# Two logarithms behind one another on ScalarE, and two masks ahead of the next head's decays on VectorE, in a gated recurrence on one core

## The chip, the core and the metric

The kernel runs on one core of a Trainium2 chip. The metric is the device time of one execution in microseconds (us); a comparison uses the median of several runs. Two kernels are told apart when they differ by more than about 0.2% of the time.

## The reference

The program is a model of four layers on 512 tokens of width 1024: an attention layer with a short convolution, a gated recurrence, and two further layers with a feed-forward part. The change touches the gated recurrence alone. It has 8 heads and two directions (forwards and backwards), 128 keys and 128 values a head, 512 tokens behind a context of 256. Of the reference this is what it computes, cut to what matters:

```python
def forget_terms(z, lb):
    lb = jnp.clip(lb.astype(jnp.float32), 0.0, 1.0).reshape(C_HEADS, 1, C_KEY_DIM)
    log_f = jnp.logaddexp(jnp.log(lb), jnp.log1p(-lb) + jax.nn.log_sigmoid(z))
    k = (1 - lb) * jax.nn.sigmoid(-z)
    return k, log_f
...
    b = jnp.cumsum(log_f, axis=3)
    k_state = k * jnp.exp(b_last - b)
    decay = jnp.exp(b_last[:, :, :, 0, :])
...
        def step(s, xs):
            q_n, k_n, v_n, b_n, qi_n, ks_n, d_n = xs
            o_inter = jnp.einsum('bhcd,bhde->bhce', qi_n, s)
            diff = b_n[:, :, :, None, :] - b_n[:, :, None, :, :]
            w = jnp.exp(jnp.where(tri, diff, -jnp.inf))
            scores = jnp.einsum('bhcd,bhsd,bhcsd->bhcs', q_n, k_n, w)
            o_n = o_inter + jnp.einsum('bhcs,bhse->bhce', scores, v_n)
            return d_n[..., None] * s + jnp.einsum('bhcd,bhce->bhde', ks_n, v_n), o_n
```

With the inputs given here the bound `lb` is 0, so the logarithm of a decay is log_sigmoid(z). The kernel gets it as min(z, 0) - ln(1 + exp(-|z|)): an absolute value, an exponential and a logarithm on ScalarE, and the rest on VectorE.

## The kernel before

The recurrence stands in `stage_c`. Each engine has its own program there, written out by hand, and runs it strictly in order; semaphores join them. No scheduler moves anything.

**Turns.** Every engine loops over turns t = 0 to 9. In turn t the projections of head t are made (five tiles, t below 8), head h = t-1 is scanned, and head t-2 gets its last scaling. The five tiles of a turn are z of direction 0, z of direction 1, q, and then two more: i and i (the values of two heads) in an even turn, g and g (the gates of two heads) in an odd one.

**TensorE** sets the pace. In turn t it runs: `flip_keys(h)` (L1455), the first z tile, `own_states(h)` (L1468, L1471), `turn(t-2)` (L1523), the second z tile, `products(h, 0)` and `products(h, 1)` (L1495, L1502), the q tile, `chunk(h, 0)`, `products(h, 2)`, `chunk(h, 1)`, `products(h, 3)`, the fourth and the fifth tile, `chunk(h, 2)`, `chunk(h, 3)`. A `chunk` is L1512, L1513 and L1515, and only L1515 needs the masked scores of its chunk (the semaphore `summed`). A tile is made of triples L315, L316, L317, a product of operands that are split into a high and a low part.

**Weights.** A unit of weights arrives in `c_raw`. ScalarE writes its high part (L1322, in `empty`, ahead of the exponential), GpSimd then its low part (L310), and TensorE waits for that. The q tile's `empty` makes the high part of the last unit that the i tiles of an even turn need. Their first TensorE instruction is therefore behind GpSimd's L310 of that unit.

**ScalarE** in turn t: `root(t-2)`, `decay_weights(h)` (L1362), `copies(h)` (L1369, L1371), the exponentials of the query and key levels (L1407, L1409), then `empty` of the five tiles, with `key_weights(t, 0)` (L1393, L1395) behind the third and `key_weights(t, 1)` behind the fourth. `empty` of a z tile is a copy (L1332), an absolute value (L1335), the next unit's high part (L1322), an exponential (L1338) and a logarithm (L1339). An activation whose function is not in the table set that is loaded has an ACT_TABLE_LOAD ahead of it.

**VectorE** in turn t: `queries(h)` (L1202, L1203), `scale(t-2)` (L1275), `keys(h)` (L1215, L1216), `states(h)` (L1230, L1233), `weigh(h)` (L1245, L1247, L1250), `gate(t-2)` (L1285), and then for direction 0 and after it for direction 1: `decays(t, dr)` and two `masks(h, n)` (L1260 to L1266). `decays(t, dr)` waits for `absolute`, which ScalarE's logarithm raises, and its last instruction raises `exponents`; the `queries` of the next turn wait for that. `products(h, 0)` waits for `levelled`, which L1250 raises. `keys(h)` raises `levels_y`, for which ScalarE's L1409 waits.

Of the kernel before, what the change touches and what calls it, by code (L numbers as in the profile page):

```python
# [25 lines left out]
CH = 8  # L26
# [148 lines left out]
def program(nc, d):  # L175
    f32, f32r, bf16 = mybir.dt.float32, mybir.dt.float32r, mybir.dt.bfloat16
    A = mybir.ActivationFunctionType
# [3 lines left out]
    with es:  # L181
# [54 lines left out]
        def stage_sems():  # L236
            turn[0] += 1
            return sets[turn[0] % 2], sets[(turn[0] + 1) % 2]
# [835 lines left out]
        buf_t1 = [c(T), c(T)]  # L1074
# [27 lines left out]
        def stage_c():  # L1102
# [4 lines left out]
            S, N = stage_sems()  # L1107

            def rev(ap):
                return ap[:, ::-1]  # L1110
# [6 lines left out]
            def bank2(b):  # L1117
                return PS[:, b:b + 2, :].rearrange("p b n -> p (b n)")
# [10 lines left out]
            with nc.Block() as block:  # L1129
# [11 lines left out]
                def _(dve):  # L1141
                    steps = [0]

                    def link(ins):
                        steps[0] += 1
                        ins.then_inc(S.dve_step, 1)
                        dve.wait_ge(S.dve_step, steps[0])
# [14 lines left out]
                    def decays(t, dr):  # L1162

                        u = 2 * t + dr
                        z, t1, nk, b = hz[:, dr, :], buf_t1[dr], buf_nk[dr], buf_b[dr]
                        dve.wait_ge(S.absolute, u + 1)
                        if t:
                            dve.wait_ge(S.keys, u - 1)
                            dve.wait_ge(S.weights, u - 1)
                            dve.wait_ge(S.levels_y, t)  # L1170
                        nc.vector.scalar_tensor_tensor(nk, z, 0.0, t1, O.max, O.add).then_inc(S.log_k, 1)
                        dve.wait_ge(S.log_k, u + 1)
                        link(nc.vector.scalar_tensor_tensor(z, z, 0.0, t1, O.min, O.subtract))
                        if dr == 0:
                            link(nc.vector.tensor_tensor_scan(b, resets, z, 0.0, O.mult, O.add))
                        else:
                            nc.vector.tensor_tensor_scan(rev(b[:, 0:L]), resets[:, 0:L], rev(z[:, 0:L]), 0.0, O.mult,
                                                         O.add)
                            link(nc.vector.tensor_tensor_scan(rev(b[:, L:T]), resets[:, L:T], rev(z[:, L:T]), 0.0,
                                                              O.mult, O.add))  # L1180
                        link(nc.vector.tensor_tensor(t1, b, nk, O.add))
                        end = P - 1 if dr == 0 else 0
                        b4, t4 = [v[:, 0:L].rearrange("p (n c) -> p n c", c=P) for v in (b, t1)]
                        nc.vector.tensor_tensor(z[:, 0:L].rearrange("p (n c) -> p n c", c=P),
                                                b4[:, :, end:end + 1].to_broadcast([P, NB, P]), t4, O.subtract)
                        cend = T - 1 if dr == 0 else L
                        nc.vector.tensor_tensor(z[:, L:T], b[:, cend:cend + 1].to_broadcast([P, LC]), t1[:, L:T],
                                                O.subtract).then_inc(S.exponents, 1)
# [64 lines left out]
                    def masks(h, n):  # L1253

                        i = h * NB + n
                        bank = PS[:, 4 + i % 2, :]
                        dve.wait_ge(S.products, i + 1)
                        if i >= 2:
                            dve.wait_ge(S.chunk_out, i - 1)
                        nc.vector.tensor_tensor(near_prod, bank[:, P:P + NEAR * 32], near_mask, O.mult)\  # L1260
                            .then_inc(S.tree, 1)
                        nc.vector.tensor_copy(am[i % 2], bank[:, 0:P])
                        dve.wait_ge(S.tree, i + 1)
                        link(nc.vector.tensor_reduce(near_sum, near_prod.rearrange("p (l c) -> p c l", l=NEAR), AX,
                                                     O.add))
                        nc.vector.copy_predicated(am[i % 2].rearrange("p (b c) -> p b c", b=4),  # L1266
                                                  block_mask.bitcast(mybir.dt.uint32).rearrange("p (b c) -> p b c", b=4),
                                                  near_sum.unsqueeze(1).to_broadcast([P, 4, 32])).then_inc(S.summed, 1)

                    def scale(h):  # L1270

                        dve.wait_ge(S.head_root, h + 1)
                        if h:
                            dve.wait_ge(S.head_turned, h)
                        nc.vector.tensor_tensor(scaled_o.rearrange("p (n c) -> p n c", n=NB),  # L1275
                                                PS[:, 7, :].rearrange("p (n c) -> p n c", n=NB),
                                                ssq[:, 2, h, :].unsqueeze(2).to_broadcast([P, NB, P]), O.mult)\
                            .then_inc(S.head_copied, 1)
# [9 lines left out]
                    for t in range(CH + 2):  # L1288
                        h = t - 1
                        if 0 <= h < CH:  # L1290
                            queries(h)
                        if t >= 2:
                            scale(t - 2)
                        if 0 <= h < CH:
                            keys(h)
                            states(h)
                            weigh(h)
                        if t >= 2:
                            gate(t - 2)
                        for dr in range(2):  # L1300
                            if t < CH:
                                decays(t, dr)
                            if 0 <= h < CH:
                                masks(h, 2 * dr)
                                masks(h, 2 * dr + 1)

                @block.scalar
                def _(act):
                    steps = [0]

                    def link(ins):
                        steps[0] += 1
                        ins.then_inc(S.act_step, 1)
                        act.wait_ge(S.act_step, steps[0])
# [9 lines left out]
                    def empty(i):  # L1324

                        t, (kind, j) = i // 5, C_TILES[i % 10]
                        ps = bank2(2 * (i % 2))
                        act.wait_ge(S.pe_tile, i + 1)
                        if kind == "z":
                            if t:  # L1330
                                act.wait_ge(S.flipped, 3 * t)
                            nc.scalar.activation(hz[:, j, :], ps[:, 0:T], A.Copy)  # L1332
                            if t:
                                act.wait_ge(S.levels_y, t)
                            nc.scalar.activation(buf_t1[j], ps[:, 0:T], A.Abs).then_inc(S.act_out, 1)  # L1335
                            high([10 * (t // 2) + u for u in SPLIT_AFTER[i % 10]])
                            act.wait_ge(S.act_out, i + 1)
                            link(nc.scalar.activation(buf_t1[j], buf_t1[j], A.Exp, scale=-1.0))  # L1338
                            nc.scalar.activation(buf_t1[j], buf_t1[j], A.Ln, bias=1.0).then_inc(S.absolute, 1)  # L1339
                            return  # L1340
                        if kind == "q":
                            if t >= 2:
                                act.wait_ge(S.products, NB * (t - 1))
                            ins = nc.scalar.activation(hq[t % 2], ps[:, 0:L], A.Silu)
                        elif kind == "g":
                            ins = nc.scalar.activation(yh[:, t - 1 + j, :], ps[:, 0:L], A.Silu)
                        else:
                            p_ = t // 2
                            if p_ >= 2:
                                act.wait_ge(S.chunk_out, NB * 2 * (p_ - 1))  # L1350
                            n = 4 if j == 0 else 2
                            ins = nc.scalar.activation(hi[p_ % 2][:, 4 * j:4 * j + n, :],
                                                       ps[:, 0:n * 256].rearrange("p (i n) -> p i n", i=n), A.Copy)
                        ins.then_inc(S.act_out, 1)
                        high([10 * (t // 2) + u for u in SPLIT_AFTER[i % 10]])
# [1550 lines left out]
        S, N = stage_sems()  # L2906
# [188 lines left out]
```

## Time and profile before

| what | value |
| --- | --- |
| median of 3 runs | 2624.97 us (2623.14 to 2625.95) |
| profiled execution, its own time | 2623.78 us |
| its span, first to last instruction | 2622.0 us |
| TensorE busy over the span | 2365.1 us (90%) |
| VectorE busy | 1457.2 us (56%) |
| ScalarE busy | 1097.0 us (42%) |
| GpSimd busy | 157.8 us (6%) |
| mean granted TensorE clock | 0.954 |

Times in the trace are counted from the span's start. The recurrence lies between about 560 and 1017 us. A row of a timeline gives the start, the duration, the engine, the line, the operation and its tiles; brackets at its end hold the idle time of that engine ahead of the instruction and what ended it. An instruction that waits for something while it already counts as started shows a longer duration instead.

### The profile page before, as it was taken

How to read it: one execution, taken by the hardware profiler on the slowest of the kernel's cores; microseconds unless marked ns; L12 is line 12 of the kernel's file. 1: busy time of each engine (PE TensorE's matmuls, PEld its weight loads, DVE VectorE, ACT ScalarE, POOL GpSimd, SP SyncE). 2: the span in 40 equal slices, each digit the busy share in tenths (PEclk: the TensorE clock that was granted, in tenths of full speed). 3: DMA queues.
4: the chain of work that ended last, by engine and by line, in shares of the span. 5: the costliest groups of instructions: out<-in, count | busy, mean ns of one | idle time of the engine just before them, and what ended most of it. 6: DMA issues, size and time to landing. Idle time of an engine off the chain costs nothing. (4 is left out here: it accounts for less than half of the span.)

```text
span 2622.0 us, 36224 instructions
## 1 busy us (share of the span) xinstructions
PE 2365.1 (90%) x15406; PEld 1926.5 (73%) x15406; DVE 1457.2 (56%) x2166; ACT 1097.0 (42%) x1738; POOL 157.8 (6%) x70
## 2 busy tenths in 40 slices
PE   6699988948999987799899999999898899999998
PEld 3598856737888876477578888886676578888875
DVE  0413276266787965436756666536536666666344
ACT  1311165155686673413734333334325724334243
POOL 0100001032232220000000000000000000000000
PEclk7799989979999997899999999999999999999999
DMA  9411100011111111222021322222130012222212
GB/s 400 152 58 56 64 1 17 1 48 50 41 57 50 57 51 39 103 112 81 1 76 49 112 97 97 103 99 80 49 145 33 2 65 81 96 97 97 104 65 80
DMA packets 34529, 201.01 MB, mean 77 GB/s; under 512 B 3776, under 2 KB 5312, under 8 KB 14656
## 3 DMA queue, kind: packets, MB, share of 16 engines
q1 hardware_dynamic: 34368, 198.69, 21.1%
q8 instruction: 122, 2.00, 0.3%
q14 instruction: 39, 0.32, 0.0%
HBM read 196.58 MB, written 2.10 MB: 76 GB/s over the span
## 5 line engine op out<-in xcount | busy, mean ns | idle before, releaser
L315 PE MATMUL ps<-a_high,w_high 128*128 128x512 f32 (+1 forms) x1680 | 628.1, 374 | 33.0 <-DVE a_low L2051 22.7
L317 PE MATMUL ps<-a_high,w_low 128*128 128x512 f32 (+1 forms) x1680 | 619.7, 369 | 0.0
L316 PE MATMUL ps<-a_low,w_high 128*128 128x512 f32 (+1 forms) x1680 | 619.7, 369 | 0.0
L1673 DVE TENSOR_TENSOR w_low<-raw_ring,w_high 128x2048 fp32r<-128x2048 f32 x102 | 233.8, 2292 | 282.6 <-ACT w_high L1667 277.8
L315 PEld LDWEIGHTS ps<-a_high,w_high 128*128 128x128 f32 x1680 | 319.0, 190 | 94.9 <-DVE w_low L1673 17.2
L316 PEld LDWEIGHTS ps<-a_low,w_high 128*128 128x128 f32 x1680 | 319.4, 190 | 53.6 <-issue 1.9
L317 PEld LDWEIGHTS ps<-a_high,w_low 128*128 128x128 f32 x1680 | 319.4, 190 | 52.4
L1667 ACT ACTIVATE w_high<-raw_ring 128x2048 fp32r<-128x2048 f32 x102 | 195.3, 1914 | 368.6 <-PE ps L317 283.3
L315 PE MATMUL ps<-c_high,c_w_high 128*128 128x512 f32 (+1 forms) x448 | 167.2, 373 | 45.6 <-POOL c_w_low L310 42.4
L315 PE MATMUL ps<-x_high,ab_high 128*128 128x256 f32 (+1 forms) x528 | 180.6, 342 | 27.4 <-POOL x_low L331 27.2
L316 PE MATMUL ps<-x_low,ab_high 128*128 128x256 f32 (+1 forms) x528 | 179.4, 340 | 0.0
L317 PE MATMUL ps<-x_high,ab_low 128*128 128x256 f32 (+1 forms) x528 | 178.9, 339 | 0.0
L316 PE MATMUL ps<-c_low,c_w_high 128*128 128x512 f32 (+1 forms) x448 | 164.0, 366 | 0.0
L317 PE MATMUL ps<-c_high,c_w_low 128*128 128x512 f32 (+1 forms) x448 | 163.9, 366 | 0.0
L315 PEld LDWEIGHTS ps<-x_high,ab_high 128*128 128x128 f32 x528 | 101.1, 191 | 41.6 <-issue 26.5
L315 PEld LDWEIGHTS ps<-c_high,c_w_high 128*128 128x128 f32 x448 | 86.8, 194 | 60.7 <-POOL c_w_low L310 43.8
L310 POOL TENSOR_TENSOR c_w_low<-c_raw,c_w_high 128x1024 fp32r<-128x1024 f32 x42 | 111.6, 2663 | 311.1 <-ACT c_w_high L1322 311.1
L2840 DVE TENSOR_TENSOR arena<-ps,arena 128x1024 f32<-128x1024 f32 x44 | 53.8, 1224 | 134.4 <-PE ps L317 134.3
L310 DVE TENSOR_TENSOR ab_low<-ab_raw,ab_high 128x2048 fp32r<-128x2048 f32 x17 | 39.0, 2292 | 135.9 <-ACT ab_high L303 135.8
L317 PEld LDWEIGHTS ps<-x_high,ab_low 128*128 128x128 f32 x528 | 101.1, 191 | 11.1
L316 PEld LDWEIGHTS ps<-x_low,ab_high 128*128 128x128 f32 x528 | 101.3, 192 | 10.2
L317 PEld LDWEIGHTS ps<-c_high,c_w_low 128*128 128x128 f32 x448 | 86.4, 193 | 13.6
(338 smaller groups left out, 4033.5 us busy)
## 6 DMA issues: line engine op xcount, KB each, us to landing
raw_ring<-w_dram SPq DMA_DIRECT2D x112, 1024.0 KB, 4.9
ada_ring<-w_dram SPq DMA_DIRECT2D x24, 1024.0 KB, 18.0
c_raw<-wc_dram SPq DMA_DIRECT2D x48, 512.0 KB, 3.5
ab_raw<-w_dram SPq DMA_DIRECT2D x17, 1024.0 KB, 4.9
x<-xT_dram SPq DMA_DIRECT2D x1, 2048.0 KB, 22.6
out_dram<-x SPq DMA_DIRECT2D x1, 2048.0 KB, 7.2
arena<-r_dram SPq DMA_DIRECT2D x2, 992.0 KB, 7.2
raw_cb<-cb_dram SPq DMA_DIRECT2D x1, 1280.0 KB, 15.2
```

Source lines behind the costliest of these rows:

```text
L310: (nc.gpsimd if by_pool else nc.vector).tensor_tensor(self.low(n), self.raw(n), self.high(n).bitcast(f32), O.subtract)\
L315: nc.tensor.matmul(out, wh, xh, start=start, stop=False)
L316: nc.tensor.matmul(out, wh, xl, start=False, stop=False)
L317: return nc.tensor.matmul(out, wl, xh, start=False, stop=stop)
L1667: nc.scalar.activation(self.high(n), self.raw(n), A.Copy).then_inc(w_hi, 1)
L1673: nc.vector.tensor_tensor(self.low(n), self.raw(n), self.high(n).bitcast(f32), O.subtract)\
L2840: nc.vector.tensor_tensor(hs[:, j % 2, :, :], tile2(PAIR[j % 4]), rstd[:, 1, :].unsqueeze(1).to_broadcast([P, 2, L]), O.mult)\
```

## The change

In ScalarE's program the z tile's `empty` ends with the exponential. Behind the exponential of the second z tile stand now both logarithms, one for each direction, with one wait ahead of the two. In VectorE's program the first two masks of head h stand ahead of the decays of head t, and the decays of direction 1 follow those of direction 0 at once; masks 2 and 3 stay last. Nothing else changes: the same activations, the same vector instructions, the same matmuls and transfers.

```diff
                         for dr in range(2):
-                            if t < CH:
-                                decays(t, dr)
                             if 0 <= h < CH:
                                 masks(h, 2 * dr)
                                 masks(h, 2 * dr + 1)
+                            if t < CH and dr == 0:
+                                decays(t, 0)
+                                decays(t, 1)
...
                             act.wait_ge(S.act_out, i + 1)
-                            link(nc.scalar.activation(buf_t1[j], buf_t1[j], A.Exp, scale=-1.0))
-                            nc.scalar.activation(buf_t1[j], buf_t1[j], A.Ln, bias=1.0).then_inc(S.absolute, 1)
+                            ins = nc.scalar.activation(buf_t1[j], buf_t1[j], A.Exp, scale=-1.0)
+                            if j:
+                                link(ins)
+                                for b in buf_t1:
+                                    nc.scalar.activation(b, b, A.Ln, bias=1.0).then_inc(S.absolute, 1)
                             return
```

ScalarE in turn 1 before, from the exponential of the first z tile (L1338) to the table load ahead of the q tile (L1344); L1339 is the logarithm:

```order
L1338 ACTIVATE arena<-arena 128x768
L1339 ACT_TABLE_LOAD
L1339 ACTIVATE arena<-arena 128x768
L1332 ACTIVATE arena<-ps 128x768
L1335 ACTIVATE arena<-ps 128x768
L1322 ACTIVATE c_w_high<-c_raw 128x1024
L1338 ACT_TABLE_LOAD
L1338 ACTIVATE arena<-arena 128x768
L1339 ACT_TABLE_LOAD
L1339 ACTIVATE arena<-arena 128x768
L1344 ACT_TABLE_LOAD
```

The same place of the changed kernel, where the exponential is L1339, the logarithms are L1343 and the q tile's load is L1348:

```order
L1339 ACTIVATE arena<-arena 128x768
L1333 ACTIVATE arena<-ps 128x768
L1336 ACTIVATE arena<-ps 128x768
L1323 ACTIVATE c_w_high<-c_raw 128x1024
L1339 ACTIVATE arena<-arena 128x768
L1343 ACT_TABLE_LOAD
L1343 ACTIVATE arena<-arena 128x768 x2
L1348 ACT_TABLE_LOAD
```

Two of the four table loads are gone, the second exponential follows the weights' high part directly, and the first logarithm stands behind the second tile.

VectorE in turn 2, from the end of `weigh` (L1250) on, as the difference between the two programs; L1285 is `gate`, L1260 to L1266 are a mask, L1171 and L1173 begin the decays:

```order
 L1250 TENSOR_TENSOR arena<-arena 128x3584
 L1285 SCALAR_TENSOR_TENSOR arena<-ps,arena 128x512
+L1260 TENSOR_TENSOR arena<-ps,arena 128x192
+L1262 COPY arena<-ps 128x128
+L1264 TENSOR_REDUCE arena<-arena 128x32
+L1266 COPY_PREDICATED arena<-arena 128x128
+L1260 TENSOR_TENSOR arena<-ps,arena 128x192
+L1262 COPY arena<-ps 128x128
+L1264 TENSOR_REDUCE arena<-arena 128x32
+L1266 COPY_PREDICATED arena<-arena 128x128
 L1171 SCALAR_TENSOR_TENSOR arena<-arena 128x768
 L1173 SCALAR_TENSOR_TENSOR arena<-arena 128x768
```

The two masks have moved from behind the first direction's decays to directly behind `gate`.

## Rows read from the trace of the kernel before

**Rows 1.** For whom TensorE waited, 560 to 1010 us: total, times, longest.

```profile
PE ps L315 <- POOL c_w_low L310: 50.1, 7, 34.6
PE ps L1495 <- DVE arena L1250: 18.8, 7, 7.7
PE ps L1515 <- DVE arena L1266: 8.6, 10, 1.4
```

**Rows 2.** Timeline of TensorE, turns 0, 1, 3, 5, 6 and 7.

```profile
594.00 0.58 PE L315 MATMUL ps<-c_w_high,c_high 128*128 128x256 f32 x1 [6.78 <-POOL c_w_low L310]
...
647.01 0.49 PE L1515 MATMUL ps<-arena 128*128 128x128 f32 x2 [0.72 <-DVE arena L1266]
...
752.64 0.49 PE L1515 MATMUL ps<-x,arena 128*128 128x128 f32 x2
...
849.21 0.53 PE L1502 MATMUL ps<-arena 128*64 128x64 f32 x12
...
857.28 0.49 PE L1515 MATMUL ps<-arena 128*128 128x128 f32 x2 [1.39 <-DVE arena L1266]
...
895.96 0.62 PE L1495 MATMUL ps<-arena 128*32 128x32 f32 x48 [1.86 <-DVE arena L1250]
...
905.50 0.49 PE L1515 MATMUL ps<-arena 128*128 128x128 f32 x2 [1.43 <-DVE arena L1266]
...
907.88 0.49 PE L1515 MATMUL ps<-arena 128*128 128x128 f32 x2 [0.23 <-DVE arena L1266]
...
909.32 0.39 PE L315 MATMUL ps<-c_w_high,c_high 128*128 128x256 f32 x1
...
964.35 0.49 PE L1515 MATMUL ps<-x,arena 128*128 128x128 f32 x2 [0.23 <-DVE arena L1266]
```

**Rows 3.** Busy us of PE, PEld, DVE, ACT, POOL; granted clock; DMA (turns 3, 5).

```profile
743.00:753.00 10.00, 9.89 (x150) 8.11 (x150) 9.83 (x14) 6.97 (x8) 2.88 (x1) 0.83 0.20 54
...
847.00:857.00 10.00, 8.15 (x148) 6.73 (x148) 9.83 (x12) 8.43 (x9) 2.92 (x1) 1.00 0.19 55
```

**Rows 4.** Timeline of VectorE, turns 5 and 6.

```profile
848.18 0.94 DVE L1171 SCALAR_TENSOR_TENSOR arena<-arena 128x768 f32<-128x768 f32 x1
849.15 3.03 DVE L1173 SCALAR_TENSOR_TENSOR arena<-arena 128x768 f32<-128x768 f32 x1
...
855.94 0.35 DVE L1260 TENSOR_TENSOR arena<-ps,arena 128x192 f32<-128x192 f32 x1
...
859.54 0.95 DVE L1171 SCALAR_TENSOR_TENSOR arena<-arena 128x768 f32<-128x768 f32 x1
...
865.29 0.35 DVE L1260 TENSOR_TENSOR arena<-ps,arena 128x192 f32<-128x192 f32 x1
...
878.18 0.69 DVE L1275 TENSOR_TENSOR arena<-ps,arena 128x512 f32<-128x512 f32 x1 [3.47 <-ACT arena L1386]
...
885.45 0.29 DVE L1230 COPY x<-ps 128x128 f32<-128x128 f32 x1 [1.89 <-PE ps L1471]
...
889.71 6.10 DVE L1250 TENSOR_TENSOR arena<-arena 128x3584 f32<-128x3584 f32 x1
```

**Rows 5.** Timeline of GpSimd, turns 4, 5 and 6.

```profile
801.62 2.97 POOL L310 TENSOR_TENSOR c_w_low<-c_raw,c_w_high 128x1024 fp32r<-128x1024 f32 x1 [7.22 <-ACT c_w_high L1322]
...
848.45 2.92 POOL L310 TENSOR_TENSOR c_w_low<-c_raw,c_w_high 128x1024 fp32r<-128x1024 f32 x1 [5.81 <-ACT c_w_high L1322]
...
889.21 2.85 POOL L310 TENSOR_TENSOR c_w_low<-c_raw,c_w_high 128x1024 fp32r<-128x1024 f32 x1 [12.25 <-ACT c_w_high L1322]
...
905.28 2.38 POOL L310 TENSOR_TENSOR c_w_low<-c_raw,c_w_high 128x1024 fp32r<-128x1024 f32 x1 [5.70 <-ACT c_w_high L1322]
```

**Rows 6.** Timeline of ScalarE, turns 5 and 6.

```profile
848.39 1.28 ACT L1338 ACT_TABLE_LOAD   x1
849.68 0.85 ACT L1338 ACTIVATE arena<-arena 128x768 f32<-128x768 f32 x1
...
883.60 3.20 ACT L1409 ACTIVATE arena<-arena 128x3584 f32<-128x3584 f32 x1
```

## The prediction, as it was put on record

> **What bounds the kernel now.** I read three views, in this order. The first is the table of waits inside the recurrence [rows 1]. The low parts of the weights cost TensorE 50.1 us, of which the entry (34.6 us) and the first i tile (6.78 us [rows 2]) are most; the query levels (L1250) cost 18.8 us and the masks (L1266) 8.6 us, in ten waits. Second, TensorE's timeline: between these waits it works without a gap, so it is the engine that the turn waits for, and what is won on it is won in the end. The ten mask waits come in pairs of 1.6 to 1.95 us, in turns 1, 2, 5, 6 and 7, between the first and the last shown in [rows 2]; 1.43 and 0.23 us are the pair of turn 6. Turns 3 and 4 have none: L1515 at 752.64 us starts without idle time [rows 2]. There the granted clock is 0.83 of full speed over ten microseconds where turn 5 has 1.00 [rows 3], the q tile runs later by about 1.3 us, and the masks are there in time. Third, the timelines of VectorE, GpSimd and ScalarE show why the masks are late: they stand behind the decays of direction 0, 848.18 to 855.94 us, 7.76 us in turn 5 [rows 4].
>
> Two things in [rows 4, 5] carry the rest. L1173 takes 3.03 us where its neighbour L1171, of the same size, takes 0.94: GpSimd's L310 ran from 848.45 us for 2.92 us, and the vector instruction that reads two tensors of the on-chip memory stood still. I take 2.1 us for one such stall. And L1250 takes 6.10 us in turn 6 because L310 began at 889.21 us, half a microsecond ahead of it; that is what keeps TensorE's products waiting 1.86 us [rows 2].
>
> **The change part by part.**
>
> *The masks move forward.* In turn 5 L1171 starts at 848.18 us, and the second products have left TensorE at 849.21 + 0.53 = 849.74 us [rows 2, 4]. The four L1260 to L1266 of a mask take 1.2 us, two masks 2.4. The first ends, held by one GpSimd stall, near 851.0, the second near 852.2. TensorE asks for them at 857.28 - 1.39 = 855.9 us [rows 2], so both are 3.7 us early and both waits go: at most 8.6 us [rows 1].
>
> In even turns something else is late next. The i tile (L315 at 909.32 us) needs the low part that GpSimd makes from 905.28 us on, for 2.38 us [rows 2, 5]. Without the two waits TensorE would be there at 909.32 - 1.66 = 907.66 us, just when GpSimd is done; in turn 4 the same L310 took 2.97 us, with VectorE at work beside it [rows 5]. The gain of an even turn therefore lies between 1.66 and 1.66 - 0.59 = 1.07 us. VectorE is busy with decays there after the change, so I take 1.2, 0.45 less than the wait, in turns 2 and 6. Masks: 8.6 - 0.9 = 7.7 us. Turns 3 and 4 bring nothing, if the clock dips there again.
>
> *ScalarE's two logarithms.* Each pair saves two table loads of 1.28 us [rows 6] a turn, 16 in all. ScalarE has idle time behind the q tile in every turn, so this counts only where TensorE waits for it: in turn 0, where the i tile waits 6.78 us for a low part whose high part stands behind the q tile on ScalarE [rows 2]. Ahead of it one load goes and one logarithm of 0.85 us (as long as the exponential in [rows 6]) comes: 1.28 - 0.85 = 0.43 us. It is nothing if GpSimd falls behind a vector instruction there; I take 0.4.
>
> A rule of the Trainium skill prices this otherwise. The loads in the trace are followed by their activation after 1.29 us (848.39 to 849.68 us, [rows 6]). "ScalarE: Activation LUTs", section "What ACT_TABLE_LOAD costs", adds about 1.38 us of draining to each switch; by that the term of turn 0 would be about 1.8 us and the total 1.4 us more. The row shows no such gap.
>
> The other side: `absolute` of direction 0 comes later. ScalarE's second exponential can start at 848.39, without the load; with 0.85, 1.28 and 0.85 us behind it the first logarithm ends near 851.4 us. VectorE is through with the masks at 852.2, so this is hidden. If VectorE were through earlier it would wait for it, at no cost to TensorE.
>
> *What the decays lose.* In turn 5 they start at 852.2 instead of 848.2 us. Direction 0 takes 7.76 - 2.1 = 5.7 us without a stall, and the L310 behind the q tile gives it one; it ends near 860.2. Direction 1 takes 865.29 - 859.54 = 5.75 us [rows 4] and ends near 866. Then come two masks (2.4) with a stall (2.1) and the 14 `queries` (4.7) with another: 877.5 us. Before, `scale` could start at 878.18 us, after 3.47 us of idle time [rows 4]; with TensorE 1.64 us earlier it could at 876.5. So `scale` and `keys` come 1.0 us late against TensorE. Behind them VectorE has 1.89 us of idle time ahead of `states` [rows 4], and so 0.9 us are left: free. State keys and masks 2 and 3 keep margins of 0.9 us and more. In turns 2 to 3, 4 to 5 and 6 to 7 the scaling is later still, and there is more room.
>
> *An overtaking.* L1409 waits for `levels_y`, and with it the first z tile's copy, its high part and GpSimd's L310, which came 889.21 - 883.60 = 5.61 us after L1409's start [rows 5, 6]. If `keys` are 1.0 us late against TensorE, L310 comes 0.5 us behind the start of L1250 rather than 0.5 ahead of it, and L1250 would run its plain 3.88 us (6.10 less the stall and a little). The products' wait of 1.86 us would go; the low part, delayed behind L1250, would be ready just as the q tile wants it. That is worth about 1.7 us a turn, in turns 2 and 6 (in turn 4 nothing moves, since turn 3 gains nothing). The ends are 0 and 3.4 us. My delay of 1.0 us is a chain of a dozen sums and the point of decision 0.5 us, so I take one of the two, 1.7 us.
>
> The Trainium skill speaks for the upper end: "SBUF — State Buffer", section "SBUF: two separate sides", says that VectorE and GpSimd lock a shared pair of ports, that the one that starts first keeps it for the whole instruction, and that the other blocks fully. The stretched L1173 and L1250 agree with the half of it in which GpSimd is first. By that rule the term would be 3.4 us, and the sum 11.5.
>
> **Sum.** 7.7 + 0.4 + 1.7 = 9.8 us. The profiled execution of before took 2623.78 us for a span of 2622.0, so the changed one would take 2614.0. The median of the three runs lies 1.2 us higher than that execution: 2624.97 - 9.8 = 2615.2 us.
>
> **The rivals.**
>
> *The overtaking takes place in both turns, or the dips go too.* 7.7 + 0.4 + 3.4 = 11.5 us give 2613.5. If TensorE keeps its full clock in turns 3 and 4, 1.3 us each come on top: 2610.9. For it: the rows show no other difference between those turns and turn 5. Against it: the idle time removed stands behind the place where the clock falls.
>
> *The gain is partly given back.* One more GpSimd stall of 2.1 us in an odd turn makes `scale` 3.1 us late, 1.2 more than VectorE's room, and the products that much later, in three pairs of turns: 9.8 - 1.7 - 3.6 = 4.5 us are left, 2620.5. For it: stalls are decided by tenths. Against it: each L310 can hold VectorE only once, and I have counted all of them.
>
> *Nothing changes.* The masks stay late, because something else than the decays holds them. For it only that turns 3 and 4 have no wait; against it that TensorE asks 3.7 us after they can be done. 2625.
>
> *Slower.* VectorE gets so late in odd turns that the next `states`, L1250 and the products come late on TensorE. The place is L1230 in turns 2, 4 and 6, behind 1.89 us of room. It decides from about 3.6 us more delay per odd turn than I worked out on: 3.6 less 0.9 of room, times three turns, is 8.1 us. At 5 us it costs 12.3 and the kernel takes about 2629. Against it: it needs two further stalls in each such turn.
>
> **How the numbers follow.** The forecast with none, one or both overtakings within it (gains of 7 to 12 us) holds 0.62, the clock back as well 0.08, the gain partly given back 0.17, nothing 0.08, slower 0.05. The forecast gives 2615.2. About 0.2% (5.2 us) is what a measurement of this kernel can tell from no change. Faster by more: the first two and a third of the third case, 0.76; same: 0.18; slower: 0.06, with a chance for clock dips elsewhere. The range goes from the lowest case with a microsecond of spread between runs, 2610, to the middle of the partial case, 2622.
>
> **What would show it.** The waits of L1515 for L1266 are gone or below 1 us in total. L1171 of direction 0 starts 3 to 5 us later than before. ScalarE has 16 table loads less. In turns 2 and 6 TensorE's first i instruction waits for GpSimd by up to 1 us. L1250 takes 3.9 or 6.1 us in turns 2 and 6, which decides the overtaking. The wait of L1275 shrinks from 3.47 us to nothing in odd-to-even steps, while that of L1230 stays above 0. Wrong would make it: a wait of L1495 for L1250 above 1.9 us, new waits for L1371 or L310, or a clock below 0.95 in the recurrence.

## The result, and the profile after

The changed kernel took 2609.2 us (median of 5 runs, 2606.78 to 2612.85), the kernel before 2624.97 us (5 runs). The ratio is 0.994, with a 95% interval of 0.9927 to 0.9954: 15.8 us less, where 9.8 were forecast, and below the range's low end of 2610.0 us. Timed once more in a later run it took 2613.26 us beside 2624.93 for the kernel before, 11.7 us less, with a ratio of 0.9954 (0.994 to 0.9968). The two intervals overlap. The gain is there, and it is between 8 and 19 us.

First the page of the changed kernel: its span, and busy time, share and instructions of each engine.

```profile
span 2607.4 us, 36208 instructions
...
PE 2357.1 (90%) x15406; PEld 1921.9 (74%) x15406; DVE 1449.7 (56%) x2166; ACT 1075.9 (41%) x1722; POOL 165.3 (6%) x70
```

ScalarE has 1722 instructions instead of 1738: the 16 table loads. The table of TensorE's waits, 560 to 1000 us, answers to [rows 1]:

```profile
PE ps L315 <- POOL c_w_low L310: 51.1, 9, 34.6
PE ps L1499 <- DVE arena L1250: 17.2, 6, 8.0
```

No row is left for the masks. `products` is L1499 now and `chunk` L1516, L1517, L1519. The wait for L1250 stands in six turns instead of seven, and GpSimd is waited for nine times instead of seven.

The recurrence, from its first tile to the start of the stage behind it, takes 439.0 us instead of 454.6 in the two profiles. That is 15.6 us. The spans of the two profiled executions differ by 14.6 us (2622.0 and 2607.4): the stages around the recurrence, which the change does not touch, took 1.0 us longer in the second. Since TensorE's order is the same, the two can be laid side by side by the starts of each group of its instructions. The table was worked out so, from the starts in the two timelines of TensorE:

| part of TensorE's order | gain, us |
| --- | --- |
| `chunk(h, 0)` and `chunk(h, 1)`, turns 1, 2, 5, 6, 7 | 2.5 + 2.2 + 2.2 + 2.2 + 2.2 |
| the same, turns 3 and 4 | 0.2 + 0.2 |
| wait of the i tile for GpSimd, turns 2 and 6 | -1.3, -0.6 |
| wait of the products for L1250, turn 2 | 1.9 |
| products and q tile at another clock, turns 3, 4, 6 | 1.5 + 1.5 - 1.5 |
| first tile of turn 1 at another clock | 1.6 |
| turn 0 | 0.0 |
| behind the last tile (clock) | 0.9 |
| sum, before rounding | 15.6 |

Turns 3 and 4 show no wait for a mask in the kernel before, and still had a trace of one. The mask of turn 3 ended at 752.58 us, and L1515 started 0.30 us behind L1513 instead of 0.22, at 752.64 us ([rows 2]); no idle time stands in its row. These are the 0.2 us of the second row.

The first row is larger than the idle time that the view of waits had shown. TensorE's timeline of the kernel before, turn 5, and of the changed one at the same place shows why:

```profile
855.28 0.38 PE L1512 MATMUL ps<-x,arena 128*128 128x128 f32 x2
855.50 0.39 PE L1513 MATMUL ps<-arena 128*128 128x128 f32 x2
```

```profile
846.88 0.38 PE L1516 MATMUL ps<-x,arena 128*128 128x128 f32 x2
847.10 0.39 PE L1517 MATMUL ps<-arena 128*128 128x128 f32 x2
847.32 0.39 PE L1519 MATMUL ps<-arena 128*128 128x128 f32 x2
847.64 0.63 PE L1499 MATMUL ps<-arena 128*32 128x32 f32 x48
```

Without a wait the instructions start 0.22 us apart although each is shown with 0.39: they overlap. With one, L1515 of the kernel before ([rows 2]) started at 857.28 us, 1.78 after L1513, and the view calls 1.39 of that idle; 857.70 - 857.28 = 0.42 us passed until the next group, where it is now 0.32. So the group `chunk(h, 0)`, up to the next products, shrank from 2.42 to 0.76 us, 1.66 for an idle time of 1.39. Each of the ten waits cost 0.27 us more than its idle time, 2.7 us in all.

VectorE's timeline of the changed kernel, turn 5, answers to [rows 4]:

```profile
840.48 0.36 DVE L1260 TENSOR_TENSOR arena<-ps,arena 128x192 f32<-128x192 f32 x1 [0.63 <-PE ps L1506]
...
841.47 1.15 DVE L1266 COPY_PREDICATED arena<-arena 128x128 f32<-128x128 uint32 x1
...
843.52 0.31 DVE L1266 COPY_PREDICATED arena<-arena 128x128 f32<-128x128 uint32 x1
843.73 0.95 DVE L1171 SCALAR_TENSOR_TENSOR arena<-arena 128x768 f32<-128x768 f32 x1
...
867.60 0.69 DVE L1275 TENSOR_TENSOR arena<-ps,arena 128x512 f32<-128x512 f32 x1 [1.20 <-ACT arena L1390]
...
874.87 0.29 DVE L1230 COPY x<-ps 128x128 f32<-128x128 f32 x1 [1.56 <-PE ps L1475]
```

The products of this turn start at 839.33 us. The second mask is done 4.5 us later and the decays start 4.4 us behind the products' start, where it was 0.44 before (848.18 - 847.74): 4.0 us later, as worked out. The wait for the scaling is 1.20 us and not nothing. GpSimd's timeline says why. This L310 began during the `queries`, 14 short instructions end to end, and took 5.18 us: VectorE kept it off, and not the other way round.

```profile
863.48 5.18 POOL L310 TENSOR_TENSOR c_w_low<-c_raw,c_w_high 128x1024 fp32r<-128x1024 f32 x1 [3.13 <-ACT c_w_high L1323]
```

In turn 5 of the kernel before it was the other way round. GpSimd got in between two of the same 14 instructions, and L1203, of 0.42 us, took 2.63 (a row of GpSimd's timeline and one of VectorE's):

```profile
868.53 2.54 POOL L310 TENSOR_TENSOR c_w_low<-c_raw,c_w_high 128x1024 fp32r<-128x1024 f32 x1 [9.06 <-ACT c_w_high L1322]
868.72 2.63 DVE L1203 TENSOR_TENSOR arena<-arena 128x256 f32<-128x256 f32 x1
```

And the overtaking, in VectorE's and in GpSimd's timeline of the changed kernel, turns 2 and 6:

```profile
678.20 3.88 DVE L1250 TENSOR_TENSOR arena<-arena 128x3584 f32<-128x3584 f32 x1
...
879.13 6.10 DVE L1250 TENSOR_TENSOR arena<-arena 128x3584 f32<-128x3584 f32 x1
```

```profile
678.22 6.10 POOL L310 TENSOR_TENSOR c_w_low<-c_raw,c_w_high 128x1024 fp32r<-128x1024 f32 x1 [10.29 <-ACT c_w_high L1323]
...
878.96 2.52 POOL L310 TENSOR_TENSOR c_w_low<-c_raw,c_w_high 128x1024 fp32r<-128x1024 f32 x1 [10.30 <-ACT c_w_high L1323]
```

In turn 2 L1250 starts 0.02 us ahead of L310 and takes its plain 3.88 us, and L310 takes 6.10. In turn 6 L310 is ahead by 0.17 us, and it is the other way round.

### The profile page after: what moved, and what is told of

Read it like the earlier page. It is cut to its first block and busy times, and to the rows that moved or that the text cites. A ratio compares the mean times of both kernels' runs of the same rounds, so it can differ in the third digit from the quotient of the medians.

```text
span 2607.4 us, 36208 instructions
## 1 busy us (share of the span) xinstructions
PE 2357.1 (90%) x15406; PEld 1921.9 (74%) x15406; DVE 1449.7 (56%) x2166; ACT 1075.9 (41%) x1722; POOL 165.3 (6%) x70
## 5 line engine op out<-in xcount | busy, mean ns | idle before, releaser
L310 POOL TENSOR_TENSOR c_w_low<-c_raw,c_w_high 128x1024 fp32r<-128x1024 f32 x42 | 119.2, 2841 | 291.1 <-ACT c_w_high L1323 291.1
L310 DVE TENSOR_TENSOR ab_low<-ab_raw,ab_high 128x2048 fp32r<-128x2048 f32 x17 | 39.0, 2292 | 135.9 <-ACT ab_high L303 135.8
```

The source lines that it names most:

```text
L310: (nc.gpsimd if by_pool else nc.vector).tensor_tensor(self.low(n), self.raw(n), self.high(n).bitcast(f32), O.subtract)\
```

## The experiments

**VectorE's edit alone (e1_masks).** ScalarE's program stays that of before.

```diff
                         for dr in range(2):
-                            if t < CH:
-                                decays(t, dr)
                             if 0 <= h < CH:
                                 masks(h, 2 * dr)
                                 masks(h, 2 * dr + 1)
+                            if t < CH and dr == 0:
+                                decays(t, 0)
+                                decays(t, 1)
```

> VectorE's edit alone (the first two masks ahead of both decays), ScalarE as before with its logarithms apart. Theory A: the whole gain comes from the masks no longer standing behind the first decays; the ten waits of TensorE for L1266 go, each worth its idle time and about a quarter of a microsecond of restart, 11.6 us together, less 1 to 2 us of waiting for GpSimd in even turns. Expected 2610 to 2615 us. Theory B: the pairing of the logarithms carries a good part (table loads saved on ScalarE): then 2618 us or more.

Measured: 2614.1 us, ratio 0.9959 (0.9946 to 0.9971), in theory A's span. The waits for masks are gone from its trace, and the pairs of `chunk` take what they take in the changed kernel. Its recurrence takes 445.1 us, 6.1 more than the changed kernel's. Of that 1.9 are the overtaking of turn 2, which it misses (L310 is 0.17 us ahead there), 1.6 the first tile of turn 1, 0.7 turn 0; the rest is clock and GpSimd in even turns. Its interval and the changed kernel's overlap.

**ScalarE's edit alone (e2_logs).**

```diff
-                            link(nc.scalar.activation(buf_t1[j], buf_t1[j], A.Exp, scale=-1.0))
-                            nc.scalar.activation(buf_t1[j], buf_t1[j], A.Ln, bias=1.0).then_inc(S.absolute, 1)
+                            ins = nc.scalar.activation(buf_t1[j], buf_t1[j], A.Exp, scale=-1.0)
+                            if j:
+                                link(ins)
+                                for b in buf_t1:
+                                    nc.scalar.activation(b, b, A.Ln, bias=1.0).then_inc(S.absolute, 1)
```

> ScalarE's edit alone, VectorE as before. Theory A: the first decays now wait for a logarithm that ends some 3 us later against TensorE's products, so the masks behind them come 3 us later too: TensorE waits about 3 us more in each of 7 turns, about 20 us slower than before, some 2643 us. Theory B (saved table loads are worth something by themselves): not slower than before.

Measured: 2645.8 us, ratio 1.0076 (1.0063 to 1.0089): slower by 20 us, the time that theory A gives. From its table of TensorE's waits:

```profile
PE ps L1518 <- DVE arena L1266: 20.4, 11, 6.3
PE ps L1498 <- DVE arena L1250: 11.1, 6, 1.9
```

The waits for masks grew by 11.8 us and not by 20, and not evenly: L1518 waited 6.3 us in turn 1, 3.8 in turns 4 and 6, and in turns 2, 3, 5 and 7 about 1.0 and 0.6. The rest of the 17.4 us by which the recurrence grew is mostly a lower clock, in the products or the q tile of turns 2, 3, 5 and 7 and behind the long waits of turns 1, 4 and 6. So the cause was named and the size met in part by luck. Saving table loads is worth nothing where the result is wanted earlier. The edit is harmless only behind the masks.

**GpSimd gives way to L1250 (e3_yield).** To the changed kernel comes one wait, on a semaphore that VectorE raises just ahead of L1250.

```diff
                     for n in range(UC["c_out"] + 2):
+                        t = 2 * (n // 10) + (n % 10 == 7)
+                        if n % 10 in (2, 7) and 1 <= t < CH:
+                            pool.wait_ge(S.key_sums, t)
                         c_stream.split_low(pool, n, by_pool=True)
```

> The changed kernel, and GpSimd's low part of the unit behind the first z tile waits for key_sums, which VectorE raises just ahead of L1250. Theory A (whoever of VectorE and GpSimd starts first keeps the other off): L1250 or the L1245 ahead of it are stretched in no turn, TensorE's wait of 1.85 us for L1250 goes in the five turns that still have it, and the low part is ready about when the q tile wants it: 8 to 9 us less than the changed kernel, 2600 to 2602 us. Rival: the low part comes too late for the q tile and gives 1 to 2 us back in each turn: no gain over the changed kernel.

Measured: 2602.72 us, ratio 0.9915 (0.9902 to 0.9929), 6.5 us below the first median of the changed kernel (10.5 below its second) and a little above theory A's span. The recurrence takes 431.9 us, 7.1 less. `L1250` is L1253 here. VectorE's and GpSimd's timelines in turn 6, and the row of TensorE's waits for it:

```profile
877.14 3.88 DVE L1253 TENSOR_TENSOR arena<-arena 128x3584 f32<-128x3584 f32 x1
```

```profile
878.43 4.84 POOL L310 TENSOR_TENSOR c_w_low<-c_raw,c_w_high 128x1024 fp32r<-128x1024 f32 x1 [13.98 <-ACT c_w_high L1326]
```

```profile
PE ps L1502 <- DVE arena L1253: 8.0, 1, 8.0
```

One wait is left, that of the last turn, which has no tile to cover it. The five others took 1.93 us each with them. Some is given back: in turns 4 and 6 the i tile waits longer for GpSimd (2.3 us for `products(h, 3)` and the wait together in turns 2, 4 and 6, where the changed kernel has 2.3, 2.0 and 1.6), and behind the fourth and fifth tile of odd turns 0.5 us appear.

**The next high part ahead of the Silu (e4_high_first).** In the changed kernel, for the q tile only.

```diff
-                            ins = nc.scalar.activation(hq[t % 2], ps[:, 0:L], A.Silu)
+                            high([10 * (t // 2) + u for u in SPLIT_AFTER[i % 10]])
+                            nc.scalar.activation(hq[t % 2], ps[:, 0:L], A.Silu).then_inc(S.act_out, 1)
+                            return
```

> The changed kernel, and in the q tile's empty the high part of the next unit stands ahead of the Silu. Theory A: in even turns the fourth tile waits for that unit's low part, which comes 0.5 us earlier: about 2 us less than the changed kernel over turns 0, 2, 4, 6, some 2607 us. Rival: the turn's length is set elsewhere by then, or the low part now falls on another vector instruction: no difference.

Measured: 2611.07 us, ratio 0.995 (0.9937 to 0.9963): no difference that can be measured from the changed kernel. The profile shows where it went. Turn 0 is 2.5 us shorter (the high part also comes ahead of the Silu's table load). The i tile of turn 2 comes 1.05 us earlier against the products ahead of it, those of turns 4 and 6 only 0.2 and 0.1. The clock took 1.6 in the first tile of turn 1, and in turns 3 and 4 products and q tile ran 1.3 to 1.4 us slower each. The recurrence takes 439.7 us, 0.6 more than the changed kernel's. So the rival was right in its outcome, and in this profile the cause was the clock, which neither named.

**The kernel before with GpSimd giving way (e6_before_yield).** The edit of e3_yield, nothing else.

> The kernel before with the one addition that GpSimd waits for key_sums. Theory A: the clock falls in products and q tile only behind TensorE's wait of 1.85 us for L1250. That wait goes in turns 2 to 7 (11.6 us), so no turn dips, and turns 3 and 4 now show the pair of waits for masks that the others have (2.2 us each). The masks come no earlier against the products, so their waits grow by what the products come earlier, up to 1.9 us a turn, and eat most of the gain: between 2614 and 2625 us. Theory B (dips come anywhere, with no tie to that wait): turns 3 and 4, or others, still have a q tile of 6.9 us.

Measured: 2644.68 us, ratio 1.0077 (1.0064 to 1.009), 20 us slower, far outside what I gave. What theory A says of the q tile came out: no turn has a slow one. The rest did not. TensorE's waits, and VectorE's timeline behind L1253 in turn 5:

```profile
PE ps L1518 <- DVE arena L1269: 29.5, 7, 4.3
```

```profile
858.65 0.74 DVE L1288 SCALAR_TENSOR_TENSOR arena<-ps,arena 128x512 f32<-128x512 f32 x1
859.31 2.49 DVE L1174 SCALAR_TENSOR_TENSOR arena<-arena 128x768 f32<-128x768 f32 x1
861.83 3.19 DVE L1176 SCALAR_TENSOR_TENSOR arena<-arena 128x768 f32<-128x768 f32 x1
...
869.75 1.73 DVE L1269 COPY_PREDICATED arena<-arena 128x128 f32<-128x128 uint32 x1
```

I had let the delayed L310 vanish. It runs as soon as L1253 is done and stops the next vector instruction that reads two tensors, and that is the first decay; the next L310 stops the second, as one did before, and a third stops the mask itself (L1269, 1.73 us instead of 0.30). In this order the masks stand behind the decays, so TensorE, which comes 1.9 us earlier, waits 4.3 us instead of 1.4. With the masks ahead of the decays the same stalls fall on work that nobody waits for. The two edits need each other.

The waits are not the whole loss. At each of the seven the granted clock fell, as the windows view shows for turn 5 (clock third from the end, 0.50), and the products and the `chunk` behind the wait ran at it: `chunk(h, 1)` took 1.58 us instead of 0.87.

```profile
872.70:876.00 3.30, 3.30 (x74) 2.71 (x76) 3.23 (x4) 0.17 (x1) 0.00 (x0) 0.50 0.39 142
```

By the starts of the groups this is some 12 us over the seven turns, two thirds of the 18.4 us by which the recurrence grew.

**The kernel before and the changed one once more (before_again, after_again).**

> The kernel before, unchanged, once more with a profile. If the clock falls by chance, other turns than 1, 3 and 4 show it; if the places are fixed by the program, the same. In either case q tiles of 6.9 us only in turns whose products waited 1.85 us for L1250.

Measured: 2628.95 us in one run, recurrence 455.3 us. Slow products and q tiles stand in turns 2, 4 and 7 here, in turns 3 and 4 in the first profile: the places change from one execution to the next. The first tile of turn 1 is slow in both. Turn 3, with its full clock, has the waits for masks that it lacked in the first profile, and in turn 7 the slow q tile leaves 0.11 us of them:

```profile
757.11 0.49 PE L1515 MATMUL ps<-x,arena 128*128 128x128 f32 x2 [1.40 <-DVE arena L1266]
```

This execution took 5.2 us more than the first profiled one, and its recurrence 0.7.

> The changed kernel, unchanged, once more, timed beside the others. If its gain over the sum that I can price (about 11.6 us from the mask waits, less 1.9 for GpSimd in even turns, and up to 1.9 for the overtaking in turn 2) was 4 us of fewer clock dips by chance, the median here is 2611 to 2615 us; if the dips are fewer by the change, 2609 again. The overtaking in turn 2 was decided by 0.02 us and may be missing here.

Measured: 2613.26 us, ratio 0.9954 (0.994 to 0.9968); recurrence 439.0 us, with the overtaking of turn 2 again (by 0.02 us) and one slow q tile, in turn 6, as in the first profile. The median lies in the span for chance, and the profiled execution, at 2609.22 us, is that of the first time: the profile does not show what the slower ones of the five lost.

**Giving way in odd turns alone (e7_yield_odd).**

```diff
-                        if n % 10 in (2, 7) and 1 <= t < CH:
+                        if n % 10 == 7 and 1 <= t < CH:
```

> The changed kernel, and GpSimd waits for key_sums in the odd turns alone (1, 3, 5, 7). Theory A (the clock in the products and the q tile falls only behind TensorE's wait of 1.85 us for L1250): a q tile of about 6.9 us can stand in turns 4 and 6 (and 2, if it isn't overtaken there), never in 3, 5 or 7; and the gain over the changed kernel is 3 times 1.9 us: 2604 to 2606 us. Theory B (dips come anywhere): an odd turn shows one.

Measured: 2605.37 us, ratio 0.992 (0.9907 to 0.9934). The waits are gone in turns 3, 5 and 7, and turns 4 and 6 happened to be overtaken. The time in theory A's span is therefore partly luck: five waits went and not three, and turn 2 took 1.9 us for its wait and 1.3 for its clock back. One turn kept the wait, turn 2, and it is the one whose products and q tile are slow (TensorE's timeline, and the windows view of 684 to 694 us with the granted clock third from the end, 0.83):

```profile
683.77 0.62 PE L1502 MATMUL ps<-arena 128*32 128x32 f32 x48 [1.86 <-DVE arena L1253]
```

```profile
684.00:694.00 10.00, 10.00 (x196) 8.27 (x183) 9.16 (x16) 6.45 (x8) 2.37 (x1) 0.83 0.18 56
```

**Both together (e5_high_first, e5_again).** To e3_yield comes the high part ahead of the tile's own activation, for the q and the i tiles:

```diff
+                        if kind != "g":
+                            high([10 * (t // 2) + u for u in SPLIT_AFTER[i % 10]])
...
                         ins.then_inc(S.act_out, 1)
-                        high([10 * (t // 2) + u for u in SPLIT_AFTER[i % 10]])
+                        if kind == "g":
+                            high([10 * (t // 2) + u for u in SPLIT_AFTER[i % 10]])
```

> The kernel in which GpSimd waits for key_sums, and the next units' high parts stand ahead of the tile's own copy or Silu for the q and i tiles. Theory A (the fourth tile of an even turn, the i tile of turn 0 and the first tile of an odd turn wait for a chain high part, low part, so 0.5 us less ahead of it counts in full): 2.5 us less in turn 0, 0.5 us in turns 2, 4, 6 each and 0.5 us in turns 1, 3, 5, 7 each, some 6 us less than 2602.7, that is 2597 us. Rival (what is won at these places is lost to lower granted clock in the products and the q tile): 2600 to 2603 us.

Measured: 2594.79 us, ratio 0.9889 (0.9873 to 0.9905), 2 us below theory A's 2597; recurrence 424.3 us.

> The kernel of run e5_high_first unchanged, timed beside the other two. The profile gives 424 us for the recurrence against 439 of the changed kernel; if this holds, about 2595 us again and a ratio to before of 0.989.

Measured: 2593.86 us, ratio 0.9875 (0.9861 to 0.9888). This is the fastest version, some 31 us less than the kernel before. Against e3_yield turn 0 is 2.5 us shorter (2.8 in e5_high_first), the even turns 1.06 us each and the odd ones 0.4; turns 5 and 7 are also 0.5 us shorter behind their last tiles, and the first tile of turn 1 runs 1.7 us slower. Its table of waits shows what is left:

```profile
PE ps L315 <- POOL c_w_low L310: 45.6, 9, 34.6
PE ps L1505 <- DVE arena L1253: 7.9, 1, 7.9
```

**The logarithms apart again, in this fastest version (e8_logs_apart).** ScalarE's edit undone, the diff of e2_logs read backwards.

> The kernel of run e5_high_first with ScalarE's logarithms apart again, as in the kernel before. What the pairing is worth where no overtaking is decided by hundredths: theory A, only turn 0 (one table load less and one logarithm more ahead of the q tile's high part): 0.5 to 0.8 us slower than e5_again. Theory B (the pairing carries what the kernels with and without it differ by, some 3 us): 3 us slower or more.

Measured: 2598.02 us, ratio 0.9891 (0.9878 to 0.9905), beside 2593.86 for e5_again. The intervals overlap in part. In the profiles turn 0 is 2.4 us longer (1.35 for the wait of the i tile, and 0.9 behind it, where the low clock lasted twice as long) and the wait of the i tile 0.65 us in each of turns 2, 4 and 6, less 1.6 us that the first tile of turn 1 wins. Theory B is nearer: the pairing is worth about 3 to 4 us here, more in turn 0 than the one load less, in part by the clock, and something in even turns, where another instruction of VectorE now runs when L310 arrives. How much of the last is chance was not tried.

## Why the prediction was wrong

*The masks.* The mechanism was right, and e1_masks shows it alone: with the masks ahead of the decays all ten waits go. VectorE's decays start 4.0 us later, and no new wait of TensorE for VectorE comes of it. The term was mis-sized, in the step "both waits go: at most 8.6 us". Idle time is not what a wait costs: the groups of `chunk` shrank by 11.6 us. Ten times 0.27 us is the overlap and restart lost at each wait, and 0.4 the two turns whose wait was too short to be shown.

*GpSimd next in even turns.* Right in place, too small in size: 1.9 us in turns 2 and 6 instead of 0.9 (waits of 1.24 and 0.55 us, where up to 1 was forecast). TensorE comes there 0.5 us sooner than its idle times had let me work out, for the same reason as above, and L310 took 3.1 us in turn 2, more than the 2.97 that I had as the bound. Part of it is the overtaking's: e1_masks, without it in turn 2, has a wait of 0.81 us there.

*Turn 0.* The wait did shrink by 0.8 us (6.78 to 5.98), but the tiles behind it ran 0.5 us slower and the ones ahead 0.3: nothing was left of 0.4. Against e1_masks and the second profile of the kernel before, turn 0 is 0.7 and 0.8 us shorter, so the nothing is partly chance. With the drain that the Trainium skill adds ("ScalarE: Activation LUTs", "What ACT_TABLE_LOAD costs") the estimate would have been 1.8. The changed kernel's trace does not agree either: in turn 0 the load of L1343 starts at 587.15 us, 0.03 behind the exponential, and the logarithm 1.29 later.

*The overtaking.* It took place in one of two turns and brought 1.9 us, 1.5 net of the 0.4 that the i tile of that turn then waits longer for GpSimd, where I took one at 1.7. The size was right, by luck: my way to it was not. I had `scale` a microsecond late because each L310 was to stop VectorE once. It did not: during the `queries` VectorE kept L310 off for 2.8 us. Four such trains meet an L310 in each profile: in the kernel before, three of them had let it in, in the changed one none did. No run tells what decides it. L310 at 6.10 us beside a plain L1250 in turn 2 agrees with the rule of the Trainium skill, "SBUF — State Buffer", "SBUF: two separate sides", that the second to start is blocked, in the half of it that the rows I had read did not show. The point of decision was missed by 0.17 us in turns 4 and 6 and met by 0.02 in turn 2. e3_yield forces the order and shows the mechanism: L1253 takes 3.88 us in each turn, and five waits go.

*The clock.* This is the step that failed: "Turns 3 and 4 bring nothing, if the clock dips there again", with the clock's return given 0.08. It did not dip there again: from 734 to 744 us, turn 3 of the changed kernel, the granted clock is 1.00, where it was 0.83 [rows 3]:

```profile
734.00:744.00 10.00, 8.15 (x156) 7.03 (x156) 9.27 (x13) 7.33 (x8) 2.39 (x1) 1.00 0.33 100
```

In the two profiles the recurrence won 4.0 us by the clock, 1.5 of it in the middle turns, 1.6 in turn 1, 0.9 at the end. I had held it against a return that the removed idle time stands behind the place. That is so, and the idle time that goes with a slow tile stands ahead of it. Counted over the profiles of all kernels in turns 2 to 7, a turn whose products waited 1.86 us for L1250 had a slow products or q tile in 17 of 40 cases, and a turn without that wait in 0 of 38. e7_yield_odd and e6_before_yield were made to break this and did not. The masks' waits come behind that place, and no run shows that taking them away brings the clock back. The change reaches that place only in turn 2, which was not slow in the first profile of the kernel before either, so the 1.5 us of the middle turns are not shown to be its doing. The places of the other slow tiles differ between two executions of the kernel before.

I had also missed that the two losses stand in for each other. A turn of the kernel before loses 2.2 us to the waits for masks, or 1.7 to 1.8 us to the clock and what is then left of them (before_again, turns 3 and 7). In the changed kernel a turn loses the clock's part, 1.2 to 1.6 us, or nothing. So slow tiles hardly change the time of the kernel before, and a turn that keeps its clock after the change gains 1.7 to 2.2 us, whichever it was before. The changed kernel, in turn, loses 1.2 to 1.6 us of its gain with each slow tile.

How much of the first measurement's 15.8 us and of the second's 11.7 is this chance, the profiles do not tell. Both profiled executions of the changed kernel took 2609.2 us, with the same slow tile. And most of the difference between profiled executions arises outside the recurrence: over the 13 profiles it began between 562.0 and 566.8 us, and what follows it took 1603.8 to 1607.1, though no edit touches either part.

The first tile of turn 1 stays open. It is slow by 1.6 us in eight profiles and not in five, the same in both profiles of before, of the changed kernel and of the fastest one. The edits do not sort it in a way that I can name: e3_yield, e7_yield_odd and e8_logs_apart have it fast, e4_high_first and e5_high_first slow. No run here tells what decides it.

So the sum should have read 11.6 - 1.9 + 1.9 + 0 = 11.6 us, and 4.0 for a clock that I could not have priced exactly but should have put into the range. The 11.6 alone give 2613.4 us, inside the range. Of the 5.8 us between the forecast 9.8 and these 15.6 the clock is 4.0, the masks net of GpSimd's part 2.0, the overtaking 0.2 and turn 0 less 0.4.

## What to carry to other kernels

Price a wait of TensorE by the distance of the starts around it against the same place without one, not by the idle time that a view gives: here a wait of 1.4 us cost a fifth more than its idle time and one of 0.25 twice as much, while the 1.86 us ahead of the products cost 1.93. Add what the clock does at a wait: it fell during or just behind each wait for masks of 3.8 to 6.3 us. Where an engine runs strictly in order, put the work that another engine waits for ahead of the work that only the next round needs, and then see on which of VectorE's instructions the stalls by GpSimd fall. A stall that costs 2 us in front of a result is free behind it, and one wait on the right semaphore decides which.

## What the hardware showed that was not expected

- Which of VectorE's L1250 and GpSimd's L310 is held up is decided by which starts first, and 0.02 us are enough: L1250 took 3.88 us with L310 at 6.10, or 6.10 with L310 at 2.52. A run of short vector instructions can keep GpSimd off as well (5.18 us for an L310 of 2.4, turn 5 of the changed kernel), or let it in (2.63 us for an L1203 of 0.42, turn 5 of the kernel before).
- Behind an idle time of 1.86 us and the small products TensorE ran slower in 17 of 40 turns, and in none of 38 without that idle time. In each of the 17 the granted clock was 0.83 over the ten microseconds from the products' start, that is 2.4 GHz for about two thirds of them and 1.2 GHz for one. The idle time itself cost 1.93 us, the clock behind it 1.2 to 1.6 us where it fell. At the waits for masks of 3.8 us and more the granted clock fell to 0.50, during the wait or just behind it, in all ten cases (seven in e6_before_yield, three in e2_logs). In the five microseconds behind those of 1.5 us and less it was at its full level each time.
- Twenty microseconds were lost by each of two edits (e2_logs, e6_before_yield) that are worth some 3 to 4 and 7 us where the masks stand ahead of the decays.
